# Modulation rows, norms, merges and rotary halves of a two-layer backbone, reordered: the swapped halves travel by transfers on GpSimd's queue

## The reference

```python
sh1, sc1, g1, sh2, sc2, g2 = split(silu(cond) @ ada_w + ada_b, 6)      # one row for context, one for latent
h = rmsnorm(x, norm1_g) * (1 + sc1) + sh1
na, swa, fu, df = project(h, w_in)
branches = [neighbourhood(na), windowed(rope(swa)), fourier(fu), differential(rope(df))]
up = [b @ w for b, w in zip(branches, w_branch)]
x = x + g1 * (sum(sigmoid(h @ w_gate + b_gate) * up) @ w_o)
h2 = rmsnorm(x, norm2_g) * (1 + sc2) + sh2
a, b = split(h2 @ w_ffn_in)
x = x + g2 * ((silu(a) * b) @ w_ffn_out)
```

## Time and profile before

| what | us |
|---|---|
| median of the runs shown | 2357.11 |
| the profiled execution's own time | 2355.65 |
| its span, first to last instruction | 2353.9 |
| PE busy (share of the span) | 2265.0 (96%) |
| DVE busy | 941.3 (40%) |
| ACT busy | 711.5 (30%) |
| GpSimd busy | 0.2 (0%) |
| mean granted clock of TensorE | 0.988 |

### The profile page before, as it was taken

One profiled execution on the slowest core, in us unless ns is written; L12 is line 12 of the kernel. 1 busy time (PEld: TensorE's weight loads), 2 busy tenths in 40 slices (PEclk: granted clock), 3 DMA queues, 4 the chain that ended last, 5 costly groups with the idle time before them and its releaser, 6 DMA issues.

```text
span 2353.9 us, 37119 instructions
## 1 busy us (share of the span) xinstructions
PE 2265.0 (96%) x15562; PEld 2145.8 (91%) x15562; DVE 941.3 (40%) x1712; ACT 711.5 (30%) x1059; POOL 0.2 (0%) x4
## 2 busy tenths in 40 slices
PE   5999999999999999999989999999999999999997
PEld 3899898888988999999989989988899899999997
DVE  4114545656444222222351254456644523222234
ACT  4223344434323221122232233433433322212221
POOL 0000000000000000000000000000000000000000
PEclk8999999999999999999999999999999999999998
DMA  6533231111433332222444233111123122212221
GB/s 270 211 135 102 90 95 49 46 49 50 145 107 104 129 112 81 67 73 76 148 161 176 84 106 104 58 46 51 46 95 143 54 80 71 94 58 71 78 79 67
DMA packets 65040, 227.18 MB, mean 97 GB/s; under 512 B 6560, under 2 KB 11168, under 8 KB 64800
## 3 DMA queue, kind: packets, MB, share of 16 engines
q1 hardware_dynamic: 64928, 225.59, 28.5%
HBM read 217.57 MB, written 6.55 MB: 95 GB/s over the span
## 4 chain that ended last, share of the span: by engine, by line
PE 88%; DVE 6%; DMA 2%; issue 2%; ACT 1%; SPq 0%; DVEq 0%; ACTq 0%
PE lp L537 74%; PE ss L701 4%; PE ss L683 2%; PE ss L595 1%; PE ss L662 1%; DMA wst<-wo 1%; DVE st L1271 1%; PE ss L603 1%; DVE tmp L1230 1%; DVE mg L1234 1%; DMA adae<-adb 1%; DVE prob L1297 1%; PE ss L780 1%; PE ss L810 1%; PE ss L669 0%
## 5 line engine op out<-in xcount | busy, mean ns | idle before, releaser
L537 PE MATMUL lp<-H,wr 128*128 128x320 f32 x9600 | 1486.9, 312 | 26.4 <-DVE H L1186 8.5
L537 PEld LDWEIGHTS lp<-H,wr 128*128 128x128 f32 x9600 | 1421.6, 189 | 56.7 <-issue 50.9
L1177 DVE TENSOR_TENSOR wr<-wst,wr 128x1024 fp32r<-128x1024 f32 (+2 forms) x236 | 318.8, 1351 | 458.9 <-ACT wr L903 457.6
L903 ACT ACTIVATE wr<-wst 128x1024 fp32r<-128x1024 f32 (+2 forms) x236 | 272.4, 1155 | 434.2 <-PE lp L537 419.8
L537 PEld LDWEIGHTS lp<-G,wr 128*128 128x128 f32 x2112 | 309.8, 188 | 0.8 <-issue 0.8
L537 PE MATMUL lp<-G,wr 128*128 128x320 f32 x2112 | 310.6, 310 | 0.0
L537 PE MATMUL lp<-BR,wr 128*128 128x320 f32 x960 | 165.5, 318 | 9.3 <-DVE wr L1177 7.5
L537 PEld LDWEIGHTS lp<-BR,wr 128*128 128x128 f32 x960 | 145.8, 191 | 14.9 <-issue 9.7
L1202 DVE SCALAR_TENSOR_TENSOR x<-lp,mod,x 128x128 f32 (+1 forms) x144 | 54.5, 434 | 227.5 <-PE lp L537 227.5
L701 PEld LDWEIGHTS ss<-V,pts 128*128 128x128 f32 x720 | 90.9, 191 | 15.9 <-ACT pts L961 8.7
L1488 DVE TENSOR_TENSOR tmp<-lp,tmp 128x640 f32<-128x640 f32 x44 | 36.3, 825 | 170.6 <-PE lp L537 170.6
(11 more groups left out here) (136 smaller groups left out, 1145.9 us busy)
## 6 DMA issues: line engine op xcount, KB each, us to landing
wst<-wff SPq DMA_DIRECT2D x88, 512.0 KB, 3.5
wst<-wgu SPq DMA_DIRECT2D x64, 640.0 KB, 4.0
sm<-adb SPq DMA_DIRECT2D x17, 2048.0 KB, 8.6
wst<-win SPq DMA_DIRECT2D x36, 512.0 KB, 3.6
wst<-wfa SPq DMA_DIRECT2D x16, 768.0 KB, 4.3
bt<-bias SPq DMA_DIRECT2D x32, 320.0 KB, 3.3
wst<-wfb SPq DMA_DIRECT2D x16, 640.0 KB, 3.9
adae<-adb SPq DMA_DIRECT2D x4, 2048.0 KB, 20.2
```

What stands on the lines that cost most here:

```text
L537: mm = pe.matmul(out[:, h, 0:TH], w[wi], act[:, ai, k, h * TH:(h + 1) * TH], start=first and i == 0, stop=last and i == 2)
L903: act.activation(wr[:, s, 0, 0:w], wst[:, s, 0:w], ACT.Copy).then_inc(w_hi[s], 1)
L1177: ve.tensor_tensor(wr[:, s, 1, 0:w], wst[:, s, 0:w], wr[:, s, 0, 0:w].bitcast(F32), ALU.subtract).then_inc(w_lo[s], 1)
```

## The change

1. `modulate` issues 16 matmuls of 256 columns instead of 8 of 512: the four groups of 32 rows hold four quarters of the 1024 channels, and the four parts of the contraction add up in PSUM. ACT's copy into `grow` is 128 x 256.
2. `turn_group` is two transposes of 128 x 128. `modulation` reads their columns with strides (four DVE operations instead of two where it takes two groups).
3. Norms: the square of the last block is not added on DVE; PE sums the seven others first and that one behind them, into the same columns. The diagonal matrices are gone: the spread is five transposes of the reciprocals, read as 128 equal columns. Norm 1 has the same form as norm 2, with a gain block ahead of each low part; `rstd` and its copy are gone. In layer 0 the gain step stands behind the first modulation on DVE.
4. At norm 2 of both layers and norm 1 of layer 1, the first `modulate` stands ahead of the last pair of chunks of W_O or OUT_B; the second one stands behind the spread.
5. The rotary matmul is gone. GpSimd's queue writes each of the seven chunks to DRAM in two transfers (14 of them), waits for all, and loads them back with the halves exchanged, seven loads into `tmp[:, 0]`, each one after the chunk before is done. DVE takes load n at step p = n + 2, behind the maxima (three operations; the sign is a column `nsg`).
6. `merge` of the jobs of step p stands behind `sums` of step p, ahead of the low parts. Before, it stood behind the outputs of step p + 1, ahead of the maxima.

```diff
 def modulate(rows, units, q):
-    for h in range(2):
-        for j in range(4):
-            mm = pe.matmul(rows[32 * j:32 * j + 32, h, :], cds[:, 4 * q + j, :],
-                           units[j][:, h * 512:(h + 1) * 512], start=(q == 0), stop=(q == 1))
+    for k in range(4):
+        for j in range(4):
+            mm = pe.matmul(rows[32 * j:32 * j + 32, 0, 0:GQ], cds[:, 4 * q + k, :], units[k][:, j * GQ:(j + 1) * GQ],
+                           start=(q == 0 and k == 0), stop=(q == 1 and k == 3))
 def turn_group(n, col):
-    for c in range(KD):
-        mm = pe.matmul(sflat[1][:, col + 2 * c:col + 2 * c + 2], grow[:, c * P:(c + 1) * P], sel,
+    for h in range(2):
+        mm = pe.transpose(sflat[1][:, col + h * P:col + h * P + P], grow[:, h * P:h * P + P], ident)
...
 def norm_sum(n):
-    pe.wait_ge(sqs, n)
+    pe.wait_ge(sqs, n * SQS + SQS)
     for t in range(TILES):
-        mm = pe.matmul(ss[0][:, 0, t:t + 1], sqacc[:, t * P:(t + 1) * P], ones[:, 0:1], start=True, stop=True)
+        pe.matmul(ss[0][:, 0, t:t + 1], sqacc[:, t * P:(t + 1) * P], ones[:, 0:1], start=(t == 0), stop=False)
+    pe.wait_ge(sq, n * SQ + SQ)
+    for t in range(TILES):
+        mm = pe.matmul(ss[0][:, 0, t:t + 1], tmp[:, 3, t * P:(t + 1) * P], ones[:, 0:1], start=False,
+                       stop=(t == TILES - 1))
 def norm_spread(n):
+    pe.wait_ge(inverse, n + 1)
     for t in range(TILES):
-        pe.wait_ge(diag, n * TILES + t + 1)
-        mm = pe.matmul(sflat[0][:, t * P:(t + 1) * P], ones, rstd[:, t * P:(t + 1) * P], start=True, stop=True)
+        mm = pe.transpose(sflat[0][:, t * P:(t + 1) * P], rt[:, t:t + 1].to_broadcast([P, P]), ident)
...
+@block.gpsimd
+def _(po):
+    for l in range(L):
+        for n, (c, w) in enumerate(TURNS):
+            chunk = IN_A + NV_TM if c == SWA_K else c
+            po.wait_ge(drained[chunk % 2], 1 + l * PER_DR + chunk // 2 + 1)
+            to = rq[n].rearrange("(b i r) t -> i b r t", i=2, r=w)
+            for i in range(2):
+                po.dma_start(to[i], qk[:, c, NCTX:T]).then_inc(st_r, 16)
+        po.wait_ge(st_r, 32 * len(TURNS) * (l + 1))
+        po.wait_ge(br_lo, l * PER_BR + 2)
+        for n, (_, w) in enumerate(TURNS):
+            if n:
+                po.wait_ge(roped, l * len(TURNS) + n)
+            po.dma_start(tmp[:, 0, 0:NLAT], rq[n].rearrange("(b r) t -> b r t", r=2 * w)[:, w // 2:w // 2 + w, :])\
+                .then_inc(ld_t, 16)
...
 for p in range(NP + 1):
-    if 1 <= p <= len(TURNS):
-        pe.wait_ge(pt_out, l * NF + F_OF[p - 1] + 1)
-        n = p - 1
-        pe.matmul(ss[0][:, 0, :], con[:, TURNS[n][1]:TURNS[n][1] + P], qk[:, TURNS[n][0], NCTX:T],
-                  start=True, stop=True).then_inc(rot, 1)
...
-    if 1 <= p <= len(TURNS):
-        rotate(l, p - 1)
     if p:
         outputs(l, p - 1)
-    if 1 <= p < NP:
-        merge(l, ups_of(p - 1))
     if p < NP:
         maxima(l, p)
-    if 1 <= p <= len(TURNS):
-        rotated(l, p - 1)
+    if 0 <= p - TURN_AT < len(TURNS):
+        rotated(l, p - TURN_AT)
     if p < NP:
         sums(l, p)
+        if p < NP - 1:
+            merge(l, ups_of(p))
         jobs_lo(l, ups_of(p))
```

More of the change, by code:

```diff
@@ L264, in build @@
         h_hi = sem("h_hi")
+        SQ, SQS = KD, KD - 1
+        MODS_AT = [n + 1 for n in range(2 * L)]
         a_f = sem("a_f")
@@ L836, in _ @@
                 modulate(ss[1], four(sm), 0)
-                norm_sum(l * 2 * KD + 2 * KD)
+                for s in range(2):
+                    weights(l, W_O, KD // 2 - 1, s)
+                    chunk(l, W_O, KD // 2 - 1, s, H, range(KD))
+                norm_sum(2 * l + 1)
+                norm_spread(2 * l + 1)
                 quad_in(1, 2)
                 modulate(ss[1], [smc[:, 0, :], smc[:, 1, :], smc[:, 2, :], smc3[:, 0, :]], 1)
-                norm_spread(2 * l + 1)
                 for ff, out, inner in ((FF_A, OUT_A, S_GA), (FF_B, OUT_B, S_GB)):
@@ L876, in _ @@
                             chunk(l, out, j, s, G, range(UNITS[out]), ready=None if s else inner)
-            norm_sum(L * 2 * KD + KD)
+                    with pe.Fori(0, KD // 2 - 1) as j:
+                        outward(j)
+                    if out == OUT_B and l + 1 < L:
+                        pe.wait_ge(mods, MODS_AT[2 * l + 2])
+                        quad_in(0)
+                        modulate(ss[1], four(sm), 0)
+                    outward(KD // 2 - 1)
+            norm_sum(2 * L)
             norm_spread(2 * L)
@@ L907, in jobs_hi, with normed_hi @@
                     weight_hi(behind(l, GATE, n // 2, n % 2))
-            def h_hi_part(l, k):
-                if k % 2 == 0:
-                    act.wait_ge(norm_x, l * 2 * KD + k + 1)
-                    act.activation(xn[:, k, 0:NCTX], xn[:, k, 0:NCTX], ACT.Identity, bias=mod[:, k, 0:1],
-                                   scale=am[:, 0, k, 0:1])
-                    own.step(act.activation(xn[:, k, NCTX:T], xn[:, k, NCTX:T], ACT.Identity,
-                                            bias=mod[:, k, 1:2], scale=am[:, 0, k, 1:2]))
-                else:
-                    act.wait_ge(v_f, odd_h(l, k))
-                act.activation(H[:, 0, k, :], xn[:, k, :], ACT.Copy).then_inc(h_hi, 1)
+            def normed_hi(n, shift):
+                for k in range(KD):
+                    act.wait_ge(norm_x, n * KD + k + 1)
+                    act.activation(H[:, 0, k, 0:NCTX], xn[:, k, 0:NCTX], ACT.Identity, bias=mod[:, shift + k, 0:1])
+                    act.activation(H[:, 0, k, NCTX:T], xn[:, k, NCTX:T], ACT.Identity, bias=mod[:, shift + k, 1:2])\
+                        .then_inc(h_hi, 1)
             def gate_tanh(l, jobs):
@@ L990, in grow_copy @@
                     act.wait_ge(group_turned, n - 1)
-                act.activation(grow[:], rows[:, :, :].rearrange("p a b -> p (a b)"), ACT.Copy).then_inc(grow_out, 1)
+                act.activation(grow[:], rows[:, 0, 0:GQ], ACT.Copy).then_inc(grow_out, 1)
             for l in range(L):
@@ L1008, in _ @@
                     act.wait_ge(ada_round, rounds_late(l) + 2)
-                for k in range(KD):
-                    h_hi_part(l, k)
+                normed_hi(2 * l, 0)
                 if l:
@@ L1343, in _ @@
             ve.wait_ge(ld_c, 16)
-            own.step(ve.tensor_reduce(sel, ident.rearrange("p (j r) -> p r j", j=4)[:, 0:2, :], AX.X, ALU.add))
-            for k in range(KD):
-                sum_square(k + 1, k % 2)
+            for k in range(SQS):
+                sum_square(0, k, k % 2)
             for l in range(L):
@@ L1360, in _ @@
                     early(0)
-                for k in range(KD + 2):
-                    if l and k < KD:
-                        normalised(k, rstd[:])
-                    if k < KD and k % 2:
-                        odd(l, k)
-                    if k >= 2:
-                        h_lo_part(l, k - 2)
+                normed(2 * l, 0, 0)
                 for c in range(IN_A + IN_B):
@@ L1504, in _ @@
                         g = AG_L - 1
-                        modulation(KD * (AG_E + g), KD, late + AG_L + (l + 1 < L), MODS_LATE + 2 * KD * g, mod_out)
+                        modulation(KD * (AG_E + g), KD, late + AG_L + (l + 1 < L), MODS_LATE, mod_out)
                         ve.wait_ge(mod_out, AG_L * (l + 1))
-                    sq0 = l * 2 * KD + 2 * KD if out == OUT_B else None
+                    nth = 2 * l + 2 if out == OUT_B else None
                     if out == OUT_B and l + 1 < L:
```

189 lines of the change are left out of this document (86 added, 103 removed).

## The result

The changed kernel takes 2327.28 us (median of four runs, 2325.14 to 2332.58); the kernel before took 2357.74 beside it. The ratio is 0.9874, with a 95% interval of 0.9854 to 0.9893: faster by 30 us. The forecast was 2307 in a range of 2295 to 2333, faster by 50. The sign and the range held; 20 us of the gain did not come, and the rest of this document is about where they are.

A forecast was written before the change was run, and what follows sets the result against it. PE bounds the kernel, holding 88% of the chain. Terms -14.6 - 12.0 - 13.4 - 3.0 - 2.4 - 4.5 + 0.4 = -49.5 took 2355.65 to 2306.1, 2307.6 on the median's scale: forecast 2307 us, range 2295 to 2333.

The forecast's parts named there:

- Rival A: Differential steps: the merge's lateness only changes places, delaying outputs and PE's next scores; gain 0 to 3, about 2318; chance 0.15.
- Rival C: Behind the norms the half clock lasts longer: +2.5 us at three places, 2315; chance 0.10.
- B: Modulates bound by their instructions, floor 0.105 us each: +1.5 per call, +26 for 17, time 2333; chance 0.08.
- Turn groups: Ten calls between chunks: two transposes at 0.22 us replace 1.68 us on PE, -14.6 us.
- Rotary: Rotary matmul leaves PE: 0.86 us each, seven per layer, 14 in all, -12.0 us.
- What the transfers need: DRAM stores and loads for the rotary: waits cost 0, as loads take 3.3 to 4.8 us, under 8.
- Merges: Differential steps: merge behind the sums frees PE from waiting, -6.7 us per layer, -13.4 for both; bounds 0 and -18.6.
- Norms: Norm 2 twice and norm 1 of layer 1: -1.0 us each, -3.0 in all; bounds +2 and -3 each.
- Last norm: Final norm, no modulate: transposes and handover -1.5 us, the dropped add -0.83, together -2.4 us.
- start: Start of layer 0: first product near 43 us instead of 47.54, -4.5 us; bounds -2 and -6.
- the condition on the prediction's bound: Layer 0's second pair of modulates: -3.0 us if the adaLN weights have landed by then, bound -1.5 if not.
- Modulate: Fourteen calls between chunks, same columns in twice as many instructions: 1.88 against 1.85 us each, +0.4 us.

## Why the prediction was right, and what in it was off

The time lies in the range, but not for the reasons that made the range. Its high end was put together from rivals A, C and half of B; of these only C came, in part. What brought the time there is a cost that the sum had at nothing (point 3), and that it was no larger is luck.

1. **Turn groups** (forecast -14.6): right. Two transposes are 0.22 on the path. With rows in time, W_IN is 5.0 and 3.6 shorter (kernel with held stores), three turn groups being 4.4. In the changed kernel itself 0.8 is left of the 8.8 that the six turn groups in W_IN stand for; the rows' waits took the rest.
2. **Rotary** (-12.0): right in the steps, -5.2 and one matmul more in each layer.
3. **What the transfers need** (0): this is the step that failed, and with it most of the 20 us. The prediction asked whether the stores are done before the first load, and they were. It did not ask what else goes through the DMA engines while ten stores of 256 KB are under way, nor what SP's queue is issuing then; it treated each queue as its own. Behind the Fourier part the stores cost 6.6 and 7.3 (from the runs in the order of the drains), in W_IN 5.2 and 2.7 (150.94 to 145.73 and 144.77 to 142.11). Measured as a whole: 16 us, by the medians of the kernel with held stores (the stretches add up to more, as the traced execution of the changed kernel lies 5.3 above its median). The loads' own cover was sized well: 7.7 us against 8, landing in 3.9 to 6.6.
4. The Trainium skill's "SBUF — State Buffer", section "Who interferes with whom", has GpSimd's transfers wait for their descriptors while DVE holds the ports that the two share; with figures from that page's section "A bandwidth-pool intuition that's wrong (but worth ruling out)" the prediction estimated up to 7.3 us for a load. The loads landed in 5.7 (median), beside 3.1 for 320 KB of bias tiles on SP's queue in the same stretch. That is within the estimate; no run here tells whether DVE held the descriptors up.
5. **Merges** (-13.4): -10.1. The term was mis-sized in one place: the wait of 1.49 for a tanh was added to the 7.8 of the sixteen steps, though it lies inside them. Without it, 7.8 - 2.6 = 5.2 per layer, against 5.06 and 5.03. Rival A did not come to pass in the steps. In the time, alone, the merge is worth 4.8 (6.6 with W_O's wait away): the rest went into half-clock stretches behind it.
6. **Norms** (-3.0): some -0.3. At norm 2, from the start of W_O's fourth-last chunk to that of FF_A's third, it is 56.13 and 55.72 us against 57.13 and 57.11, so -1.0 and -1.4, near the -1.0 forecast, but by another way. The first product comes no earlier (39.78 and 39.51 us after that start, 39.63 in both layers before): the gap is 1.8 shorter (11.38 to 9.56 from the last product of W_O in layer 0), and the modulate that moved ahead costs that much. The gain is that FF_A's first products no longer run at half clock. What holds them now is DVE: its gain blocks and low parts, 0.92 and 0.93 a pair, fill the chain from 699.51 to 713.74 but for 1 us of ACT, and FF_A's first 96 products take 16.35 us where the next 96 take 14.19. The end of that stretch in the chain:

```profile
712.80 0.94 DVE H L1185 x2
...
713.78 1.14 PE lp L564 x6
```

Norm 1 of layer 1 lost 2.1 (82.72 to 84.86 from OUT_B's first product to W_IN's, with both modulates in both). The step that failed there: the second modulate "now lies in PE's wait for DVE" and "stays hidden". At norm 1 its rows lie in the memory that ACT's high parts are written to, so ACT waited 5.04 for it, and it ran at half clock, 3.31. The five transposes of the spread were also taken too cheap: 0.76 at full clock and 1.33 at half; from reciprocal to gain step it is 1.42 at half clock and 0.85 at full (the kernel with the second modulate in the gap), where 0.75 was forecast.
7. **The clock.** Rival C was a part of the truth: the modulate that moved away had kept PE busy in the gap, and in the changed kernel most of the sum's second half (2.14 us), the spread and the second modulate ran at 0.50 granted, 1.2 GHz. In all five traced kernels that have the second modulate behind the spread it takes 3.20 to 3.64 us at each of the three norms; in the two that have it in the gap, 1.93 at each. The sum's second half is slow in some of the five traces (up to 2.29) and takes 1.28 in others:

```profile
696.00:697.00 1.00, 1.00 (x6) 1.00 (x6) 0.65 (x1) 0.32 (x1) 0.00 (x0) 0.50 0.00 0
...
700.00:701.00 1.00, 1.00 (x16) 0.43 (x12) 1.00 (x3) 0.38 (x2) 0.00 (x0) 0.50 0.34 135
701.00:702.00 1.00, 1.00 (x16) 0.42 (x12) 0.77 (x3) 1.00 (x4) 0.00 (x0) 0.50 0.00 0
...
703.00:704.00 1.00, 1.00 (x8) 1.00 (x8) 1.00 (x3) 0.37 (x2) 0.00 (x0) 1.00 0.28 29
```

(windows of the changed kernel, norm 2 of layer 0; the seventh number is the clock). In exchange FF_A's first products ran at full clock (1.00 from 703 us on), where they had had 0.50 before. At norm 1 there was no such exchange: W_IN's first products ran at 0.50 from 1194 to 1197 us too.

8. **Last norm** (-2.4) and **start** (-4.5): from the 2880 products behind the last turn group to the end it is 440.17 and 436.98, -3.2. The start gave -2.5 in these two traces; in the traces of kernels that leave it alone it takes 45.65 to 48.59, in those with the new one 44.26 to 45.40, so that the size is open by a microsecond or more. The modulates of the second pair are bound by the fourth load of rows, as the condition on the prediction's bound said:

```profile
36.59 3.44 PE L622 MATMUL lp<-adae,cds 128*32 128x256 f32 x32 [2.31 <-DMA adae<-adb]
```

9. **Modulate** (+0.4): 1.86 against 1.85. Right.

## What to carry to other kernels

A transfer that is off the path is not free: ask at which point of the program it will be in flight, what else is in flight then, and which engine's queue stands behind the transfer that it delays. A list of waits on an in-order queue runs at the pace of its latest member: sort it by when each member is ready, or hold it until the queues are empty. When PE's work is moved out of a gap, the gap's own work can slow down with the clock, and work moved into it can push the slow stretch behind it; price a removed wait as its length plus the slow stretch that followed it. And where DVE paces the products behind a norm, a first product that starts earlier ends nothing earlier.

## What the runs showed of the hardware that was not expected

- SP's issue of two transfers took 3.99 us instead of 0.81 while GpSimd's ten stores of 256 KB were under way, and five small ones 4.81 instead of 2.58; with the stores held back it took 0.81 and 2.48, and a 512 KB weight beside them 13.4 to land instead of 3.6.
- A wait of PE at W_O's second pair costs more than its length: behind 2.67 and 3.43 us of wait (layers 0 and 1 of the kernel with the second modulate in the gap) the next products ran at a granted clock of 0.50, and removing these waits won 5.7 and 5.0. It need not: behind 2.15 us of wait in layer 0 of the changed kernel the same 12 products took 2.02.
- The same instructions in the same gap run at full clock in one kernel (1.92 for the second modulate of norm 1 before) and lose it in another (2.43 and 2.86) that differs only elsewhere; alone, the moved merge lost half of its gain that way.
